# A relative-position table built by 16 shifted transfers, and a 31-tap convolution with all four channel tiles on VectorE

## The chip, the cores and the metric

The kernel runs on one core of a Trainium2 chip. The metric is the device time of one execution in microseconds (us).

## What is computed

Two transformer-like blocks on 256 tokens of width 2048, all float32. The first block has two layers; each projects `x` to 7168 columns, runs three mixers on them (a causal depthwise convolution over 31 taps and 512 channels, a gated recurrence, a retention), projects back, and ends with a feed-forward part of width 8192. The second block has an even layer (neighbourhood attention, a two-way delta rule, attention to a memory) and an odd layer (differential attention). The two places that the change touches are these:

```python
def conv_mixer(a_in, gate_in, w_dw, b_dw, ln_g, ln_b):
    u = a_in.astype(jnp.float32) * jax.nn.sigmoid(gate_in.astype(jnp.float32))
    y = lax.conv_general_dilated(u, w_dw.astype(jnp.float32)[:, None, :], window_strides=(1,),
                                 padding=[(CONV_WIDTH - 1, 0)],
...
                                 feature_group_count=D_CONV) + b_dw
    return jax.nn.silu(layer_norm(y, ln_g, ln_b))

def neighbourhood_attention(q, k, v, rpb):
...
    dr = key_rows - r[:, None] + (NA_WIN_H - 1)
    dc = jnp.clip(c[None, :] - c[:, None], -(NA_WIN_W - 1), NA_WIN_W - 1) + (NA_WIN_W - 1)
    bias = rpb[:, dr[:, None, :, None], dc[None, :, None, :]]
    s = s + bias[None].astype(jnp.float32)
    s = jnp.where(col_ok[None, None, None, :, None, :], s, -jnp.inf)
```

The 256 tokens are a grid of 4 rows by 64 columns, so every query sees all 4 rows and 16 of the 64 columns, and `bias[head, query, key]` depends only on the row difference and the column difference. `rpb` is 6 heads by 15 by 31 numbers.

## The kernel before

**The weight stream.** All big products are units of 512 output columns. A unit is 8 blocks; a block is 256 rows by 512 columns of a weight, 512 KB. For each block SyncE loads it (L221) into one of 8 buffers, ScalarE copies it to a rounded high part `w_hi` (L228), VectorE subtracts to get the low part `w_lo` (L235; called the split below), and TensorE runs 12 matmuls of 128x512 with them (L250 to L252). SyncE loads a block as soon as TensorE has finished the block 8 before it. ScalarE and VectorE run `AHEAD = 6` blocks ahead of TensorE in their program: where TensorE has done n blocks, their text stands behind split n + 6. Position n below means n blocks done in the stage's own count.

**Work woven in.** In a mixer stage each engine's program is written out by hand, `run(n)` standing for the next n blocks of the stream and `upto(run, n)` for all up to position n, with the mixer's own instructions between them. All engines wait for one another through counters (`wait_ge(*k.name.next(who))`, raised by `.then_inc(*k.name.up())`).

**The convolution** (`dve_conv`, `pool_conv`, `pe_conv`, both layers of the first block). Channels lie on partitions in four tiles of 128, 256 tokens along the free axis. VectorE does three tiles: for each tap three multiply-adds of 128x256 (L899), then `run(1)`. It begins at position 5. Behind taps 22, 26 and 27 stand larger steps of the next mixer's gates (`dve_hgrn_gates`, L1086 to L1109), which ScalarE answers with Abs, Exp and Ln (`act_hgrn_gates`). GpSimd does the fourth tile meanwhile, two instructions for a tap (L843, L845), from the time of VectorE's first tap. TensorE transposes the gates' input at position 26 (L935) and, at position 38 in the first layer and 42 in the second, waits for the last tap and for GpSimd, and transposes the result back (L874). VectorE's normalisation and everything later in the mixers follows from that.

**The table** (`pe_even_inputs`, `dve_even_inputs`, even layer). `na_bias` is 128 partitions (two grid rows of 64 query columns) by 6 heads, 2 token tiles, 4 key rows and 64 key columns. TensorE transposes the 90x31 table (L1978) at position 51, and then multiplies it with shifted windows of a constant 31x191 band, 32 products of 31x128 by 42 columns at position 53 and 32 at position 58 (L1993); each picks, for one key column, the entry of every query column. VectorE copies the table (L2069) and moves each half from PSUM to `na_bias`, adding the column mask, in 12 instructions on 64 partitions (L2089). At position 61 it divides (L1849) and scales the heads (L1855), which raises `att_scaled`; TensorE, at position 64, waits for that before it transposes queries and keys (L2118) for the attention. ScalarE squares heads at positions 48 to 58, takes their root, and applies Silu to the gate (L1924). In the attention VectorE adds `na_bias` to the scores of each head (L1774).

`na_bias` shares its SBUF with the delta rule's buffers, which are free once VectorE has raised `dn_scaled` (after L1855 at position 47).

Of the kernel before, what the change touches and what calls it, by code (L numbers as in the profile page):

```python
# [83 lines left out]
def constants():  # L84
# [11 lines left out]
    j, v = np.arange(31)[:, None], np.arange(63 + P)[None, :]  # L96
    band = ((63 - v + 15) % 64 == j).astype(f32)
# [9 lines left out]
        "c_band": band,  # L107
        "c_window": np.concatenate([window, window], 0),
# [540 lines left out]
DVE_CONV = CONV_C // P - 1  # L649
# [11 lines left out]
def first_buffers(k):  # L661
# [43 lines left out]
    k.conv_pool, = count("conv_pool")  # L705
# [117 lines left out]
def pool_conv(pool, k):  # L823

    g = k.nc.gpsimd

    def step(ins):
        ins.then_inc(*k.pool_step.up())
        pool.wait_ge(*k.pool_step.now())

    def weight(n):
        return k.conv_w[:, DVE_CONV, n:n + 1].to_broadcast([P, SEQ])

    y = k.conv_y[:, DVE_CONV, :]
    pool.wait_ge(*k.conv_tap.next("pool"))
    k.conv_tap.next("pool", DVE_CONV * CONV_W - 1)
    step(g.tensor_tensor(y, k.conv_u[:, DVE_CONV, 0:SEQ], weight(0), ALU.mult))
    g.tensor_tensor(k.conv_work[:, 1, :], k.conv_u[:, DVE_CONV, 1:1 + SEQ], weight(1), ALU.mult)
    step(g.tensor_tensor(y, y, weight(CONV_W), ALU.add))
    for tap in range(1, CONV_W):  # L840

        if tap + 1 < CONV_W:
            g.tensor_tensor(k.conv_work[:, (tap + 1) % 2, :], k.conv_u[:, DVE_CONV, tap + 1:tap + 1 + SEQ], weight(tap + 1),  # L843
                            ALU.mult)
        last = g.tensor_tensor(y, y, k.conv_work[:, tap % 2, :], ALU.add)  # L845
        if tap + 1 < CONV_W:
            step(last)
    last.then_inc(*k.conv_pool.up())


def pe_conv(pe, k, l, run):
# [18 lines left out]
    pe.wait_ge(*k.conv_tap.next("pe", DVE_CONV * CONV_W - 1))  # L870
    pe.wait_ge(*k.conv_pool.next("pe"))
# [6 lines left out]
def dve_conv(dve, k, l, run):  # L878
# [514 lines left out]
def second_buffers(k):  # L1393
# [95 lines left out]
    k.att_scaled, k.att_gainT, k.att_gained, k.na_tableT, k.na_table_kept = \  # L1489
        later(DEPTH, k.conv_root, k.conv_linear, k.conv_done, k.h_fT, k.h_f_read)  # L1490
    k.na_toeplitz, k.na_bias_kept, k.att_turned, k.att_turn_kept, k.at_s = \
        later(DEPTH, k.h_kx, k.h_key, k.h_qT, k.h_query, k.h_cumulated)
# [4 lines left out]
    k.dn_summed, = later(DEPTH * DVE_CONV * CONV_W, k.conv_tap)  # L1497
# [253 lines left out]
def dve_attention(dve, k, maps, arrays, run=no_blocks, apart=0):  # L1751
# [15 lines left out]
    for n in range(len(maps) + 2):  # L1767
        run(apart)
        if n < len(maps):
# [3 lines left out]
            if bias is not None:  # L1773
                v.tensor_tensor(att_s[:, n % 2], scores, bias, ALU.add).then_inc(*k.dve_step.up())  # L1774
# [7 lines left out]

def even_maps(k):
# [144 lines left out]
def pe_even_inputs(pe, k, run):  # L1928
# [23 lines left out]
    for part in range(3):  # L1952
# [43 lines left out]
    pe.wait_ge(*k.na_bias_kept.next("pe"))  # L1996
# [1034 lines left out]
```

## Time and profile before

| | |
|---|---|
| time, median of 3 runs | 3681.41 us (3677.53 to 3681.42) |
| profiled execution, its own time | 3684.41 us |
| span of that execution | 3682.5 us |
| TensorE busy | 3506.1 us, 95% |
| VectorE busy | 2214.5 us, 60% |
| ScalarE busy | 1615.8 us, 44% |
| GpSimd busy | 440.9 us, 12% |
| DMA | 615.50 MB, mean 167 GB/s |

The span is from the first to the last instruction that the profiler saw. Busy time is the sum over the engine's instructions, so it says how full an engine is on average and nothing about which wait ends last at one place. In a timeline the start of an instruction minus that of the next is its real pace; its listed duration also holds the part that overlaps with the next one. Brackets give idle time before an instruction and who ended it.

### The profile page before, as it was taken

How to read it: one execution, taken by the hardware profiler on the slowest of the kernel's cores; microseconds unless marked ns; L12 is line 12 of the kernel's file. 1: busy time of each engine (PE TensorE's matmuls, PEld its weight loads, DVE VectorE, ACT ScalarE, POOL GpSimd, SP SyncE). 2: the span in 40 equal slices, each digit the busy share in tenths (PEclk: the TensorE clock that was granted, in tenths of full speed). 3: DMA queues.
4: the chain of work that ended last, by engine and by line, in shares of the span. 5: the costliest groups of instructions: out<-in, count | busy, mean ns of one | idle time of the engine just before them, and what ended most of it. 6: DMA issues, size and time to landing. Idle time of an engine off the chain costs nothing.

```text
span 3682.5 us, 44184 instructions
## 1 busy us (share of the span) xinstructions
PE 3506.1 (95%) x16538; PEld 2929.9 (80%) x16538; DVE 2214.5 (60%) x2397; ACT 1615.8 (44%) x1953; POOL 440.9 (12%) x330
## 2 busy tenths in 40 slices
PE   7899999999999997999999999999999978999999
PEld 6778778887888776877888888888888868788877
DVE  5986565555555688865655555566446553555654
ACT  4454334443434345434444443444445433355553
POOL 0625000000000061340100000000000032000100
PEclk9999999999999999999999999999989889999999
DMA  6545455555555564446656555556645300655544
GB/s 208 171 132 166 172 183 187 191 188 178 188 183 189 170 183 143 137 144 205 217 190 188 192 187 191 189 183 196 194 145 178 109 6 1 194 175 171 177 126 160
DMA packets 310634, 615.50 MB, mean 167 GB/s; under 512 B 19082, under 2 KB 19113, under 8 KB 308539
## 3 DMA queue, kind: packets, MB, share of 16 engines
q1 hardware_dynamic: 306144, 591.73, 50.4%
q0 software_dynamic: 4320, 21.34, 1.7%
q8 instruction: 127, 2.08, 0.2%
q14 instruction: 43, 0.35, 0.0%
HBM read 610.90 MB, written 2.10 MB: 166 GB/s over the span
## 4 chain that ended last, share of the span: by engine, by line
PE 84%; DVE 9%; ACT 2%; DMA 1%; POOL 1%; issue 1%; SPq 0%; DVEq 0%; ACTq 0%; POOLq 0%
PE ps_unit L250 25%; PE ps_unit L252 25%; PE ps_unit L251 25%; DVE sb_w_lo L235 3%; DVE sb_conv_y L899 3%; PE ps_mix L2322 2%; PE ps_mix L973 1%; PE ps_mix L374 1%; PE ps_mix L528 1%; DMA sb_raw<-in_w_in_dram 1%; ACT sb_w_hi L228 1%; PE ps_mix L1993 1%; PE ps_mix L2320 0%; DMA sb_raw<-in_w_ff_dram 0%; PE ps_mix L2677 0%
## 5 line engine op out<-in xcount | busy, mean ns | idle before, releaser
L235 DVE TENSOR_TENSOR sb_w_lo<-sb_raw,sb_w_hi 128x1024 fp32r<-128x1024 f32 x1120 | 1424.8, 1286 | 1028.2 <-ACT sb_w_hi L228 1023.2
L228 ACT ACTIVATE sb_w_hi<-sb_raw 128x1024 fp32r<-128x1024 f32 x1120 | 1177.9, 1059 | 1501.6 <-DMA sb_raw<-in_w_ff_dram 742.9
L250 PE MATMUL ps_unit<-sb_w_hi,sb_a_hi 128*128 128x512 f32 x3456 | 1374.7, 398 | 51.0 <-DVE sb_w_lo L235 27.2
L252 PE MATMUL ps_unit<-sb_w_hi,sb_a_lo 128*128 128x512 f32 x3456 | 1358.0, 393 | 0.0
L251 PE MATMUL ps_unit<-sb_w_lo,sb_a_hi 128*128 128x512 f32 x3456 | 1357.7, 393 | 0.0
L250 PEld LDWEIGHTS ps_unit<-sb_w_hi,sb_a_hi 128*128 128x128 f32 x3456 | 656.5, 190 | 193.7 <-DVE sb_w_lo L235 30.0
L252 PEld LDWEIGHTS ps_unit<-sb_w_hi,sb_a_lo 128*128 128x128 f32 x3456 | 655.6, 190 | 139.2
L251 PEld LDWEIGHTS ps_unit<-sb_w_lo,sb_a_hi 128*128 128x128 f32 x3456 | 656.5, 190 | 132.1
L250 PE MATMUL ps_unit<-sb_w_hi,sb_f_hi 128*128 128x512 f32 x1024 | 400.5, 391 | 0.0
L252 PE MATMUL ps_unit<-sb_w_hi,sb_f_lo 128*128 128x512 f32 x1024 | 399.2, 390 | 0.0
L251 PE MATMUL ps_unit<-sb_w_lo,sb_f_hi 128*128 128x512 f32 x1024 | 398.9, 390 | 0.0
L252 PEld LDWEIGHTS ps_unit<-sb_w_hi,sb_f_lo 128*128 128x128 f32 x1024 | 192.3, 188 | 40.2
L251 PEld LDWEIGHTS ps_unit<-sb_w_lo,sb_f_hi 128*128 128x128 f32 x1024 | 192.4, 188 | 39.5
L250 PEld LDWEIGHTS ps_unit<-sb_w_hi,sb_f_hi 128*128 128x128 f32 x1024 | 192.3, 188 | 39.3
L606 POOL TENSOR_TENSOR sb_relu<-sb_relu 128x1024 f32<-128x1024 f32 x32 | 60.7, 1896 | 1181.6 <-ACT sb_relu L588 1181.6
L358 DVE TENSOR_TENSOR sb_x<-sb_x,ps_unit 128x1024 f32<-128x1024 f32 (+1 forms) x48 | 58.6, 1221 | 109.9 <-PE ps_unit L252 109.9
L899 DVE SCALAR_TENSOR_TENSOR sb_conv_y<-sb_conv_u,sb_conv_w,sb_conv_y 128x256 f32<-128x256 f32 x180 | 112.7, 679 | 0.1
L402 ACT ACTIVATE sb_a_hi<-ps_mix 128x512 fp32r<-128x512 f32 x88 | 50.1, 596 | 127.1 <-PE ps_mix L374 127.0
L414 DVE TENSOR_TENSOR sb_a_lo<-ps_mix,sb_a_hi 128x512 fp32r<-128x512 f32 x88 | 57.6, 686 | 74.1 <-ACT sb_a_hi L402 74.1
L342 ACT ACTIVATE sb_proj<-ps_unit 128x1024 f32<-128x1024 f32 (+1 forms) x48 | 49.2, 1024 | 94.7 <-PE ps_unit L252 94.6
L625 DVE TENSOR_TENSOR sb_f_lo<-ps_mix,sb_f_hi 128x1024 fp32r<-128x1024 f32 x32 | 39.2, 1225 | 42.1 <-ACT sb_f_hi L579 42.1
L362 DVE BATCH_NORM_STATS2 sb_stats<-sb_x 128x6 f32<-128x512 f32 (+1 forms) x96 | 61.8, 685 | 3.0 <-DVE sb_x L358 0.3
(455 smaller groups left out, 2181.4 us busy)
## 6 DMA issues: line engine op xcount, KB each, us to landing
sb_raw<-in_w_ff_dram SPq DMA_DIRECT2D x512, 512.0 KB, 3.6
sb_raw<-in_w_in_dram SPq DMA_DIRECT2D x224, 512.0 KB, 3.6
sb_raw<-in_e_w_in_dram SPq DMA_DIRECT2D x112, 512.0 KB, 3.4
sb_raw<-in_o_w_in_dram SPq DMA_DIRECT2D x112, 512.0 KB, 3.5
sb_raw<-in_w_out_dram SPq DMA_DIRECT2D x64, 512.0 KB, 3.7
sb_raw<-in_e_w_out_dram SPq DMA_DIRECT2D x32, 512.0 KB, 3.7
sb_raw<-in_o_w_out_dram SPq DMA_DIRECT2D x32, 512.0 KB, 3.6
sb_raw<-in_e_w_mem_kv_dram SPq DMA_DIRECT2D x16, 512.0 KB, 3.6
```

The costliest lines, as they stand in the source:

```text
L228: k.nc.scalar.activation(k.w_hi[:, j], k.raw[:, j], ACT.Copy).then_inc(k.hi_ready, 1)
L235: k.nc.vector.tensor_tensor(k.w_lo[:, j], k.raw[:, j], k.w_hi[:, j].bitcast(F32), ALU.subtract).then_inc(k.lo_ready, 1)
L250: k.nc.tensor.matmul(acc, hi[:, kt, tokens], w_hi, start=kt == 0, stop=False)
L251: k.nc.tensor.matmul(acc, hi[:, kt, tokens], w_lo, start=False, stop=False)
L252: last = k.nc.tensor.matmul(acc, lo[:, kt, tokens], w_hi, start=False, stop=kt == KT - 1)
L358: k.nc.vector.tensor_tensor(k.x[:, :, cols], k.x[:, :, cols], k.ps_unit[:, u % 2], ALU.add).then_inc(k.evacuated, BLOCKS)
L362: last = k.nc.vector.bn_stats(k.stats[:, t, bass.ds(chunk, 1), :].rearrange("p c s -> p (c s)"), k.x[:, t, cols])
L402: k.nc.scalar.activation(k.a_hi[:, KB * g:KB * (g + 1), :], k.ps[:, g % 4, :].rearrange("p (a s) -> p a s", a=KB), ACT.Copy).then_inc(*k.t ...
L414: k.nc.vector.tensor_tensor(k.a_lo[:, part, :], k.ps[:, g % 4, :].rearrange("p (a s) -> p a s", a=KB), k.a_hi[:, part, :].bitcast(F32), AL ...
L606: k.nc.gpsimd.tensor_tensor(k.relu2[:, u % 2], k.relu[:, u % 2], k.relu[:, u % 2], ALU.mult).then_inc(k.relu2_ready, 1)
L899: ins = v.scalar_tensor_tensor(y, u, k.conv_w[:, c, tap:tap + 1], y, ALU.mult, ALU.add)
L2322: last = tensor.matmul(out[:, x, :], left[:, n, :], right[:, n, :], start=True, stop=True)
```

## The change

The 64 band matmuls, the transpose and copy of the table and the 24 masked moves out of PSUM are gone. In their place GpSimd issues 16 transfers, one for each token tile, grid row and key row; each writes 64 partitions by 6 heads by 64 columns and reads, for query column q, the 64 numbers that start q places further in a row of the table stored back to front. The key columns so stand in reverse order in `na_bias`; the mask is stored in reverse too, and the attention reads the bias from its last column backwards. VectorE adds the mask in one instruction of 128x3072 elements at position 59. In the convolution GpSimd's part is gone, and VectorE does four multiply-adds for each tap.

```diff
-DVE_CONV = CONV_C // P - 1
+CONV_TILES = CONV_C // P
...
-def pool_conv(pool, k):
...
     pe.wait_ge(*k.h_kx.next("pe"))
-    pe.wait_ge(*k.conv_tap.next("pe", DVE_CONV * CONV_W - 1))
-    pe.wait_ge(*k.conv_pool.next("pe"))
+    pe.wait_ge(*k.conv_tap.next("pe", CONV_TILES * CONV_W - 1))
...
     for tap in range(CONV_W):
-        for c in range(DVE_CONV):
+        for c in range(CONV_TILES):
...
-                dve.wait_ge(sem, done + DVE_CONV * (tap - 1) + c + 1)
+                dve.wait_ge(sem, done + CONV_TILES * (tap - 1) + c + 1)
...
+def from_last_column(bias):
+
+    last = bias[:, :, :, GRID - 1:]
+    return bass.AP(last.tensor, last.offset, [list(step) for step in last.ap[:-1]] + [[-1, GRID]])
...
+NA_BIAS = TT * 2 * GRID_ROWS * 16
+
+
+def pool_na_bias(pool, k):
+
+    rpb = k.dram["na_rpb_2"]
+    pool.wait_ge(*k.dn_scaled.next("pool"))
+    with k.nc.allow_non_contiguous_dma(reason="a window of the table for each query column"):
+        for t in range(TT):
+            for r in range(2):
+                for a in range(GRID_ROWS):
+                    row = WIN_H - 1 - (2 * t + r) + a
+                    src = bass.AP(rpb.tensor, rpb.offset + row * RPB_COLS + WIN_W - GRID,
+                                  [[1, GRID], [RPB_ROWS * RPB_COLS, HEADS], [1, GRID]])
+                    pool.dma_start(k.na_bias[r * GRID:(r + 1) * GRID, :, t, a, :], src).then_inc(*k.na_bias_in.up(16))
...
     tensor.transpose(k.ps[:, 0, 0:4], k.gain_rows[:], k.ident[0:4, 0:4]).then_inc(*k.att_gainT.up())
-    tensor.transpose(k.ps[0:RPB_COLS, 1, 0:HEADS * RPB_ROWS], k.na_rows[:],
-                     k.ident[0:HEADS * RPB_ROWS, 0:HEADS * RPB_ROWS]).then_inc(*k.na_tableT.up())
-    run(2)
...
-            last = tensor.matmul(k.ps[:, n // BIAS_PER_BANK, at:at + BIAS_COLS], pick, table, start=True, stop=True)
-        last.then_inc(*k.na_toeplitz.up())
     run.rest()
-    pe.wait_ge(*k.na_bias_kept.next("pe"))
...
+    run(59 - run.done)
+    dve.wait_ge(*k.na_bias_in.next("dve", NA_BIAS))
+    bias = k.na_bias[:].rearrange("p h t r c -> p (h t r) c")
+    v.tensor_tensor(bias, bias, k.na_window[:].unsqueeze(1).to_broadcast([P, HEADS * SEQ // P * GRID_ROWS, GRID]),
+                    ALU.add).then_inc(*k.na_bias_kept.up())
     run(max(61 - run.done, 0))
...
     g.memset(k.dn_u[:, :, SEQ + 2:DN_T], 0.0).then_inc(*k.dn_pad.up())
+    pool_na_bias(pool, k)
     pool.wait_ge(*k.dn_g_done.next("pool"))
```

Besides these, two of the eleven small loads of `pool_even_rows` are gone (the table and the band), VectorE waits for `na_bias_kept` before the attention, and the table is reversed along its last axis before the launch.

## Rows read from the trace of the kernel before

**Rows 1.** the page, its chain by line: shares of the span
```profile
PE ps_unit L250 25%; PE ps_unit L252 25%; PE ps_unit L251 25%; DVE sb_w_lo L235 3%; DVE sb_conv_y L899 3%; PE ps_mix L2322 2%; PE ps_mix L973 1%; PE ps_mix L374 1%; PE ps_mix L528 1%; DMA sb_raw<-in_w_in_dram 1%; ACT sb_w_hi L228 1%; PE ps_
```

**Rows 2.** chain that ended last, first layer: start us, us, what
```profile
95.05 2.38 DVE sb_conv_y L899 x3
...
97.43 1.69 DVE sb_w_lo L235
```

**Rows 3.** Windows: length, busy PE, PEld, DVE, ACT, POOL, then PEclk, DMA share, GB/s
```profile
91.00:152.00 61.00, 56.17 (x248) 45.05 (x247) 61.00 (x62) 25.14 (x24) 58.65 (x61) 1.00 0.57 173
152.00:172.00 20.00, 20.00 (x91) 16.42 (x90) 20.00 (x31) 1.06 (x1) 0.57 (x1) 1.00 0.61 184
192.00:216.00 24.00, 17.69 (x71) 14.13 (x69) 19.28 (x28) 14.78 (x17) 0.00 (x0) 0.86 0.39 120
...
2506.00:2508.00 2.00, 2.00 (x11) 1.65 (x10) 0.00 (x0) 2.00 (x4) 0.00 (x0) 1.00 1.02 363
2882.00:2887.00 5.00, 5.00 (x14) 3.92 (x14) 4.56 (x9) 0.00 (x0) 0.00 (x0) 0.52 0.00 0
```

**Rows 4.** VectorE timeline, first layer, GpSimd idle: start us, us, line
```profile
157.02 1.27 DVE L899 SCALAR_TENSOR_TENSOR sb_conv_y<-sb_conv_u,sb_conv_w,sb_conv_y 128x256 f32<-128x256 f32 x3
158.21 1.21 DVE L235 TENSOR_TENSOR sb_w_lo<-sb_raw,sb_w_hi 128x1024 fp32r<-128x1024 f32 x1
```

**Rows 5.** VectorE timeline, the second block's five-tap convolution
```profile
2750.26 1.23 DVE L235 TENSOR_TENSOR sb_w_lo<-sb_raw,sb_w_hi 128x1024 fp32r<-128x1024 f32 x1
2751.40 1.68 DVE L2038 SCALAR_TENSOR_TENSOR sb_dn_y<-sb_dn_u,sb_dn_w,sb_dn_y 128x256 f32<-128x256 f32 x4
2752.98 1.23 DVE L235 TENSOR_TENSOR sb_w_lo<-sb_raw,sb_w_hi 128x1024 fp32r<-128x1024 f32 x1
```

**Rows 6.** TensorE timeline, twelve matmuls apart
```profile
87.40 0.39 PE L250 MATMUL ps_unit<-sb_w_hi,sb_a_hi 128*128 128x512 f32 x1
...
90.12 0.39 PE L250 MATMUL ps_unit<-sb_w_hi,sb_a_hi 128*128 128x512 f32 x1
```

**Rows 7.** VectorE timeline, first layer, its waits and the last tap
```profile
174.66 1.23 DVE L235 TENSOR_TENSOR sb_w_lo<-sb_raw,sb_w_hi 128x1024 fp32r<-128x1024 f32 x1 [1.43 <-ACT sb_w_hi L228]
...
181.20 1.23 DVE L235 TENSOR_TENSOR sb_w_lo<-sb_raw,sb_w_hi 128x1024 fp32r<-128x1024 f32 x1 [4.13 <-ACT sb_w_hi L228]
...
197.41 1.27 DVE L899 SCALAR_TENSOR_TENSOR sb_conv_y<-sb_conv_u,sb_conv_w,sb_conv_y 128x256 f32<-128x256 f32 x3
```

**Rows 8.** line L874, the transposes back, both layers: min/median/max ns
```profile
L874 PE MATMUL ps_mix<-sb_square,sb_conv_y x16: 270/347/449, 198.8 to 1440.9; 128*128 128x128 f32 x16
```

**Rows 9.** chain that ended last, around the band matmuls
```profile
2872.34 9.93 PE ps_mix L1993 x64
2898.27 11.78 PE ps_mix L1993 x64
```

**Rows 10.** VectorE timeline, second block, around the table
```profile
2856.92 3.43 DVE L1855 TENSOR_TENSOR sb_proj<-sb_proj,sb_head_ss 128x1536 f32<-128x1536 f32 x2
...
2921.08 0.40 DVE L1849 RECIPROCAL sb_head_ss<-sb_head_ss 128x40 f32<-128x40 f32 x1
...
2927.80 0.69 DVE L1855 TENSOR_TENSOR sb_proj<-sb_proj,sb_head_ss 128x512 f32<-128x512 f32 x1
```

**Rows 11.** ScalarE timeline, gate of the attention, then copies of the stream
```profile
2898.41 1.28 ACT L1924 ACT_TABLE_LOAD   x1
...
2901.10 2.05 ACT L228 ACTIVATE sb_w_hi<-sb_raw 128x1024 fp32r<-128x1024 f32 x2
```

**Rows 12.** DMA queues and issues: KB each, median us to landing
```profile
q1 hardware_dynamic: 306144, 591.73, 50.4%
...
sb_raw<-in_e_w_in_dram SPq DMA_DIRECT2D x112, 512.0 KB, 3.4
...
sb_gain<-in_e_ln_g_dram POOLq DMA_DIRECT2D x1, 1024.0 KB, 7.7
...
sb_gw_raw<-in_e_w_in_dram POOLq DMA_DIRECT2D x1, 192.0 KB, 9.2
```

More of the change, by code:

```diff
@@ L106, in constants @@
         "c_rope": rope.reshape(SEQ, HD),
-        "c_band": band,
-        "c_window": np.concatenate([window, window], 0),
+        "c_window": np.concatenate([window, window], 0)[:, ::-1].copy(),
         "c_pairs": np.ascontiguousarray((lev + lev.transpose(2, 1, 0)).reshape(P, 7 * P)),
@@ L820, in act_conv @@
     a.activation(ca, ca, ACT.Silu).then_inc(*k.conv_done.up())
-def pool_conv(pool, k):
[L825 to L848, printed above, removed]
 def pe_conv(pe, k, l, run):
@@ L1488, in second_buffers @@
     k.gates_kept, k.even_gated = later(DEPTH, k.conv_weights, k.conv_gated)
[L1489 to L1492, printed above, removed]
+    k.att_scaled, k.att_gainT, k.att_gained = later(DEPTH, k.conv_root, k.conv_linear, k.conv_done)
+    k.na_bias_in, = count("na_bias_in")
+    k.na_bias_kept, k.att_turned, k.att_turn_kept, k.at_s = later(DEPTH, k.h_key, k.h_qT, k.h_query, k.h_cumulated)
     k.at_max, k.at_e, k.at_t, k.at_c, k.at_o = later(DEPTH, k.h_o, k.h_square, k.h_msq, k.h_root, k.h_gated)
@@ L1773, in dve_attention @@
             if bias is not None:
-                v.tensor_tensor(att_s[:, n % 2], scores, bias, ALU.add).then_inc(*k.dve_step.up())
+                v.tensor_tensor(att_s[:, n % 2].rearrange("p t (r c) -> p t r c", c=GRID),
+                                scores.rearrange("p t (r c) -> p t r c", c=GRID), bias, ALU.add).then_inc(*k.dve_step.up())
                 scores = att_s[:, n % 2]
@@ L2066, in dve_even_inputs @@
     dve.wait_ge(*k.att_gainT.next("dve"))
-    v.tensor_copy(k.att_gain[:], k.ps[:, 0, 0:4]).then_inc(*k.dve_step.up())
-    dve.wait_ge(*k.na_tableT.next("dve"))
-    v.tensor_copy(k.na_table[:], k.ps[0:RPB_COLS, 1, 0:HEADS * RPB_ROWS]).then_inc(*k.na_table_kept.up())
-    dve.wait_ge(*k.dve_step.now())
+    step(v.tensor_copy(k.att_gain[:], k.ps[:, 0, 0:4]))
     for n in (0, 2):
@@ L2074, in dve_even_inputs @@
     last.then_inc(*k.att_gained.up())
-    run(1)
-    dve.wait_ge(*k.dn_scaled.now())
-    for half in range(2):
-        run(1)
-        dve.wait_ge(*k.na_toeplitz.next("dve"))
-        for first in range(0, BIAS_ROUND, BIAS_PER_BANK):
-            n = min(BIAS_PER_BANK, BIAS_ROUND - first)
-            src = k.ps[:, first // BIAS_PER_BANK, 0:n * BIAS_COLS].rearrange("p (c h a) -> p h a c", c=n, h=HEADS)
-            keys = slice(half * BIAS_ROUND + first, half * BIAS_ROUND + first + n)
-            for t in range(TT):
-                for r in range(2):
-                    part = slice(r * GRID, (r + 1) * GRID)
-                    a = GRID_ROWS - 1 - (2 * t + r)
-                    window = k.na_window[part, keys].unsqueeze(1).unsqueeze(1).to_broadcast([GRID, HEADS, GRID_ROWS, n])
-                    last = v.tensor_tensor(k.na_bias[part, :, t, :, keys], src[part, :, a:a + GRID_ROWS, :], window, ALU.add)
-            run(1)
-        last.then_inc(*k.na_bias_kept.up())
+    run(59 - run.done)
[3 more added lines that the diff above has]
+                    ALU.add).then_inc(*k.na_bias_kept.up())
     run(max(61 - run.done, 0))
@@ L2143, in dve_even_attention @@
     dve.wait_ge(*k.even_gated.next("dve"))
+    dve.wait_ge(*k.na_bias_kept.now())
     dve_attention(dve, k, even_maps(k), k.e_att)
```

34 lines of the change are left out of this document (6 added, 28 removed).

## The prediction

> **What bounds the kernel now.** I read the chain by line first, then the chain in order of time at both places of the change, then the timelines of single engines there and the windows over them, last the DMA issues. The chain by line: half and more of it is the three matmul lines of the weight stream, and two VectorE lines follow, the split L235 and the convolution's L899 [rows 1]. So the kernel is bound by TensorE, except where something holds it up, and both edits are at such places. TensorE's own pace is 2.72 us a block: 87.40 to 90.12 for twelve matmuls [rows 6].
>
> In the convolution the chain runs through VectorE: 2.38 us for the three tiles of a tap and 1.69 for the split, 4.07 us a block [rows 2]. While that lasts GpSimd is busy for 58.65 of 61 us; from 152 on it does nothing but 0.57 us of its last tap [rows 3], and VectorE's same three multiply-adds take 158.21 - 157.02 = 1.19 us [rows 4], half of before. The split beside an idle GpSimd takes 2751.40 - 2750.26 = 1.14 [rows 5]. GpSimd's two-input instructions hold VectorE's two-input ones back, and for 15 blocks (61 us / 4.07) this sets VectorE's pace. TensorE lives on its lead of 6 blocks meanwhile and hardly idles (56.17 of 61 busy), but at the transposes back it waits for the last tap, which ends at 198.6 [rows 7], and L874 starts at 198.8 [rows 8].
>
> In the even layer the band matmuls stand on the chain with 9.93 and 11.78 us [rows 9]. TensorE is its own bound there: it does them instead of the stream.
>
> **Part 1, the convolution.** Four multiply-adds and a split are in the trace already: the five-tap convolution of the second block does just that, with GpSimd idle, from split to split 2752.98 - 2750.26 = 2.72 us [rows 5]. It is TensorE's pace to the hundredth, so VectorE neither gains nor loses on it. Along VectorE's program in layer 1:
> - 15 blocks at 2.72 instead of 4.07: 20.2 us earlier.
> - 14 later blocks with a fourth multiply-add of 1.19 / 3 = 0.40: 5.6 later; one more at tap 0: 0.4 later.
> - VectorE idles before two splits for ScalarE's gate work (1.43 and 4.13 us [rows 7]). ScalarE starts that when VectorE's L1087 is done, so it moves along; the fourth multiply-add lies inside the idle, 0.8 back.
>
> That makes 15.0, the last tap at 183.6. Can TensorE be there? It is at position 5 at 87.4 [rows 6]. 33 blocks at 2.72 are 89.8, and the gates' 12 transposes with their wait some 3 us (the 8 of L874 are of 0.27 to 0.35 us each [rows 8]): position 38 at 180.2. So it waits 3.4 us for the tap, less than now, and VectorE stays the bound. Its lag behind TensorE stays under the six blocks. What follows L874 is a chain of its own (normalise, root, Silu, scan) and moves as it is.
>
> Layer 2 has the same 15 slow blocks and the same steps of ScalarE behind VectorE's, so its transposes back, now at 1440.9 [rows 8], move by 15.0 too.
>
> One more term has only bounds. In 192 to 216 TensorE idles 6.3 of 24 us, and its granted clock is 0.86 in the mean, so part of the stretch at 1.2 GHz and not at 2.4 [rows 3]; with a shorter idle the clock may stay up, worth 0 to 24 x 0.14 = 3.4 us a layer. I take 1 each. Part 1: 15 + 15 + 2 = 32 us, range 25 to 38. GpSimd's own edit costs nothing: its next work waits for VectorE's scan, and its DMAs at the stage's head stand ahead of it as before.
>
> **Part 2, TensorE's side of the table.** The first band product starts at 2872.34, two blocks after position 51 [rows 9], so position 51 is at 2866.9 and, with 13 blocks straight, position 64 at 2866.9 + 35.4 = 2902.3. Now it comes at 2928.5: 26 us, of which 21.7 are the products and most of the rest the clock: behind them, 2882 to 2887, it is granted at 0.52, that is 1.2 GHz, with 14 matmuls where 2.72 / 12 each would give 22 [rows 3].
>
> **VectorE's side.** TensorE needs `att_scaled`, raised now at the end of the scaling, 2928.4 [rows 10]. A load lands 3.4 us after its issue [rows 12], then come 1.03 for ScalarE's copy (2.05 for two [rows 11]) and 1.14 for the split; split n + 6 is issued when TensorE is at n - 2. So VectorE reaches position 59 when TensorE is at 57 (2883.2) plus 5.6, at 2888.8; ScalarE's Silu with its table load (2901.10 - 2898.41 = 2.7 [rows 11]) falls there and pushes the copy by 1.8, as the squares before it leave ScalarE little room: 2890.6. Then the mask, 3072 elements: by the scaling's L1855, 3.43 for two of 1536 [rows 10], 3.4 us. Two splits 2.3: 2896.3. From divide to `att_scaled` is 2921.08 to 2928.4 now, 7.3 [rows 10]: 2903.6. That is behind TensorE's 2902.3, so the gain is 2928.4 - 2903.6 = 24.8. The attention then reads the bias backwards; no row has a negative step. I take 0; at half speed it would be 6 heads x 0.6 = 3.6.
>
> **The 16 transfers** are what the trace doesn't price. They may start when `dn_scaled` is up (2856.92 + 3.4 = 2860.3 [rows 10]) and are wanted at 2890.6, 30 us. Each has 384 runs of 256 bytes, 6144 in all. Lower bound, by bytes: 1.5 MB, about 1.5 of the 1 MB `gain` broadcast at 7.7 us [rows 12], under 12 us. Upper bound, each run as dear as a packet of the stream: 50.4% of 3682.5 us x 16 engines over 306144 packets is 97 ns [rows 12]; 384 runs for each engine are 37 us, in the 0.4 of the engines that the stream leaves 93 us, 62 late. Nearest row: `gw_raw`, 2048 runs of 96 bytes, lands after 9.2 us although it is queued behind that broadcast [rows 12]; three of it are 27.6, ending at 2888. I take that they are just in time. They push the stream too: in 2506 to 2508 the engines are full [rows 3]. TensorE has six blocks of lead against that, VectorE's position 59 doesn't; 2 us off. Part 2: 24.8 - 2 = 23 us, range 8 to 27.
>
> The page "DMA: Bandwidth & Descriptors" of the Trainium skill (Specifications) asks for at least 512 bytes in a run for full rate, and its fixed cost (Anatomy of one DMA) is about 2.0 us plus bytes / 436e3 per transfer. Sixteen of 98 KB one after another would by that be an estimated 36 us, 6 late, and the gain of part 2 some 17 instead of 23; `gw_raw`'s row stands against it only if they overlap, which no row here shows.
>
> **Sum.** 32 + 23 = 55. Against the profiled execution: span 3682.5 - 55 = 3627, own time 3684.4 - 55 = 3629. The median of the runs is 3.0 below that own time: 3626.
>
> **The rivals.**
> - *Transfers late, still a gain.* VectorE stands at position 59; the path from there to `att_scaled` is serial, so each us late is one lost. For: runs of 256 bytes, a full DMA system. Against: `gw_raw`. 10 to 40 late: a gain of 15 to 45, about 3650.
> - *Slower than before.* The same wait, with the transfers one after another, each as long as `gw_raw` (9.2 us): 147 us, done at 3008, 117 late, so 3681 - 55 + 117 = 3743. It decides from (30.3 + 55) / 16 = 5.3 us a transfer. Everything is behind it, since VectorE's splits wait too and TensorE starves after six blocks. Against: four small loads of the trace don't add up like that.
> - *The convolution gives little.* If VectorE's slowness were not GpSimd's doing, four tiles would take 4.07 + 0.80 = 4.87 a block and each layer lose. Against: the step to 1.19 falls where GpSimd stops, in both layers. A milder form: TensorE or ScalarE comes late at the transposes and half of the 30 us is lost, 3641.
>
> **Chances.** Forecast (gain 42 to 68) 0.68; late transfers with a gain 0.15; half the convolution 0.10; slower 0.05; no effect that shows 0.02. From no change a measurement of this kernel can tell about 0.2%, 7 us. So faster 0.93, same 0.02, slower 0.05. The range takes the forecast's own spread (sum of the parts' bounds, 3616 to 3648) and a little of the late case above it: 3612 to 3652.
>
> **What would show it.** After tap 0, L899 at 1.59 us for four and the split at 1.13, 2.72 a block from the first tap on, L874 near 184; no L1993, and the clock full from 2866 on in old time; the mask instruction of 3072 elements with no idle for a DMA before it; `att_scaled` some 37 us after position 51. The prediction is wrong if VectorE idles for `na_bias`, if the split's idle for ScalarE grows by more than a block in the convolution, or if the stream's loads land late while the 16 are in flight.

## The result, and the profile after

The changed kernel's median is 3625.77 us (four runs, 3622.23 to 3627.62) beside 3681.38 for the kernel before: a ratio of 0.9846, 95% interval 0.9835 to 0.9858. The prediction was 3626.0, in the range 3612 to 3652. The profiled execution took 3622.23 us by its own time, span 3620.4. Its line numbers differ from those of before: the split is L232 (was L235), ScalarE's copy L225 (L228), the convolution L865 (L899), the transposes back L840 (L874), the first products behind them L939 (L973), the scaling L1835 (L1855), the mask L2037, the 16 transfers L1789.

The page's chain by line answers to [rows 1]; the split and the convolution have gone from 3% each to 2%. The band matmuls are no longer in the program:

```profile
PE ps_unit L247 26%; PE ps_unit L249 26%; PE ps_unit L248 26%; DVE sb_w_lo L232 2%; PE ps_mix L2271 2%; DVE sb_conv_y L865 2%; PE ps_mix L939 1%; PE ps_mix L371 1%; PE ps_mix L525 1%; DMA sb_raw<-in_w_in_dram 1%; ACT sb_w_hi L225 1%; PE ps_mix L2269 0%; DMA sb_raw<-in_e_w_in_dram 0%; PE ps_mix L2626 0%; PE ps_mix L2606 0%
```

**The convolution.** VectorE's timeline in the first layer (start us, us, line), against [rows 2] and [rows 4]:

```profile
103.57 1.23 DVE L232 TENSOR_TENSOR sb_w_lo<-sb_raw,sb_w_hi 128x1024 fp32r<-128x1024 f32 x1
104.71 1.68 DVE L865 SCALAR_TENSOR_TENSOR sb_conv_y<-sb_conv_u,sb_conv_w,sb_conv_y 128x256 f32<-128x256 f32 x4
106.29 1.23 DVE L232 TENSOR_TENSOR sb_w_lo<-sb_raw,sb_w_hi 128x1024 fp32r<-128x1024 f32 x1
107.42 1.68 DVE L865 SCALAR_TENSOR_TENSOR sb_conv_y<-sb_conv_u,sb_conv_w,sb_conv_y 128x256 f32<-128x256 f32 x4
...
157.00 1.23 DVE L232 TENSOR_TENSOR sb_w_lo<-sb_raw,sb_w_hi 128x1024 fp32r<-128x1024 f32 x1 [1.04 <-ACT sb_w_hi L225]
...
163.55 1.22 DVE L232 TENSOR_TENSOR sb_w_lo<-sb_raw,sb_w_hi 128x1024 fp32r<-128x1024 f32 x1 [3.74 <-ACT sb_w_hi L225]
```

From tap to tap it is 107.42 - 104.71 = 2.71 us, where it was 4.07: one multiply-add more, and both lines at their quick pace. The two idle times for ScalarE were 1.43 and 4.13 [rows 7]; each is 0.39 shorter, since one multiply-add more lies inside it.

The windows of the same stretches, and those around the 16 transfers (length, busy PE, PEld, DVE, ACT, POOL, granted clock, DMA share, GB/s), answer to [rows 3]:

```profile
91.00:152.00 61.00, 61.00 (x277) 50.67 (x276) 60.74 (x111) 26.33 (x25) 0.00 (x0) 1.00 0.65 190
152.00:172.00 20.00, 20.00 (x90) 16.57 (x89) 15.18 (x24) 15.00 (x13) 0.00 (x0) 1.00 0.66 186
172.00:192.00 20.00, 14.85 (x64) 12.24 (x63) 19.86 (x31) 7.54 (x8) 0.00 (x0) 0.91 0.42 128
192.00:216.00 24.00, 22.45 (x116) 18.63 (x116) 20.29 (x16) 17.16 (x18) 8.68 (x4) 1.00 0.53 154
2820.00:2828.00 8.00, 8.00 (x37) 6.36 (x36) 4.17 (x4) 7.16 (x33) 8.00 (x13) 1.00 0.93 244
2828.00:2836.00 8.00, 8.00 (x37) 6.64 (x36) 1.91 (x5) 3.60 (x13) 1.97 (x4) 1.00 1.04 256
2836.00:2844.00 8.00, 8.00 (x37) 6.64 (x36) 4.63 (x4) 7.90 (x33) 0.00 (x0) 1.00 0.77 250
```

GpSimd is out of the first stretch, and TensorE does 277 matmuls in it where it did 248. The transposes back, line L840 over both layers, answer to [rows 8] (its columns are min/median/max ns, then the first and the last start); the second fence is TensorE's timeline at the first of them:

```profile
L840 PE MATMUL ps_mix<-sb_square,sb_conv_y x16: 270/347/445, 183.6 to 1404.8; 128*128 128x128 f32 x16
```

```profile
183.58 0.66 PE L840 MATMUL ps_mix<-sb_square,sb_conv_y 128*128 128x128 f32 x2 [5.15 <-DVE sb_conv_y L865]
```

So 198.8 became 183.6 and 1440.9 became 1404.8, and TensorE still waits 5.15 us there for the last tap.

**The table.** VectorE's timeline around it, against [rows 10]:

```profile
2815.93 3.43 DVE L1835 TENSOR_TENSOR sb_proj<-sb_proj,sb_head_ss 128x1536 f32<-128x1536 f32 x2
2819.28 1.22 DVE L232 TENSOR_TENSOR sb_w_lo<-sb_raw,sb_w_hi 128x1024 fp32r<-128x1024 f32 x1
...
2851.40 1.23 DVE L232 TENSOR_TENSOR sb_w_lo<-sb_raw,sb_w_hi 128x1024 fp32r<-128x1024 f32 x1 [2.73 <-ACT sb_w_hi L225]
2852.54 3.35 DVE L2037 TENSOR_TENSOR sb_na_bias<-sb_na_bias,sb_na_window 128x3072 f32<-128x3072 f32 x1
...
2858.08 0.40 DVE L1829 RECIPROCAL sb_head_ss<-sb_head_ss 128x40 f32<-128x40 f32 x1
...
2864.80 0.69 DVE L1835 TENSOR_TENSOR sb_proj<-sb_proj,sb_head_ss 128x512 f32<-128x512 f32 x1
2865.40 2.35 DVE L232 TENSOR_TENSOR sb_w_lo<-sb_raw,sb_w_hi 128x1024 fp32r<-128x1024 f32 x2
2867.67 2.06 DVE L2085 TENSOR_SCALAR sb_na_t<-ps_mix,sb_att_gain 128x512 f32<-128x512 f32 x3
```

The instruction behind the scaling shows when `dn_scaled` is up, 2819.3, and when `att_scaled` is up, 2865.4. That is 46.1 us, where it was 2928.4 - 2860.3 = 68.1 [rows 10]. The mask has no bracket in front: it waits for no transfer. The transfers themselves, line L1789 (issue durations in ns, first and last start, then issue to landing), and the queues from 2815 to 2860:

```profile
L1789 POOL DMA_DIRECT2D sb_na_bias<-in_na_rpb_dram x16: 653/656/697, 2819.7 to 2829.3; - x16
...
DMA to landing us min/median/max: 3.7/5.9/7.1
```

```profile
q1 hardware_dynamic: 4380, 8.44, 62.2%
q0 software_dynamic: 768, 1.57, 15.6%
...
sb_raw<-in_e_w_in_dram SPq DMA_DIRECT2D x9, 512.0 KB, 5.4
```

They are issued 0.64 us apart and all have landed by 2829.3 + 7.1 = 2836.4, 16 us ahead of the mask. On the 16 engines they take 15.6% of 45 us, 7.0 us of each engine. The stream pays some of it: for some 16 us the DMA engines are full (shares of 0.93 and 1.04) and its loads take 5.4 us to land instead of 3.4 [rows 12]. TensorE goes on without a gap in all three windows.

### The profile page after: what moved, and what is told of

It reads as the page before. It is cut to its first block, busy times and chain, and to the rows that moved or that the text cites. A ratio compares the mean times of both kernels' runs of the same rounds, so it can differ in the third digit from the quotient of the medians.

```text
span 3620.4 us, 43852 instructions
## 1 busy us (share of the span) xinstructions
PE 3467.1 (96%) x16409; PEld 2901.0 (80%) x16409; DVE 2176.0 (60%) x2435; ACT 1619.0 (45%) x1953; POOL 329.4 (9%) x220
## 4 chain that ended last, share of the span: by engine, by line
PE 86%; DVE 8%; ACT 2%; DMA 1%; POOL 1%; issue 1%; SPq 0%; DVEq 0%; ACTq 0%; POOLq 0%
PE ps_unit L247 26%; PE ps_unit L249 26%; PE ps_unit L248 26%; DVE sb_w_lo L232 2%; PE ps_mix L2271 2%; DVE sb_conv_y L865 2%; PE ps_mix L939 1%; PE ps_mix L371 1%; PE ps_mix L525 1%; DMA sb_raw<-in_w_in_dram 1%; ACT sb_w_hi L225 1%; PE ps_mix L2269 0%; DMA sb_raw<-in_e_w_in_dram 0%; PE ps_mix L2626 0%; PE ps_mix L2606 0%
## 5 line engine op out<-in xcount | busy, mean ns | idle before, releaser
L232 DVE TENSOR_TENSOR sb_w_lo<-sb_raw,sb_w_hi 128x1024 fp32r<-128x1024 f32 x1120 | 1406.6, 1268 | 1046.0 <-ACT sb_w_hi L225 1041.0
L225 ACT ACTIVATE sb_w_hi<-sb_raw 128x1024 fp32r<-128x1024 f32 x1120 | 1178.2, 1059 | 1479.2 <-DMA sb_raw<-in_w_ff_dram 741.7
L399 ACT ACTIVATE sb_a_hi<-ps_mix 128x512 fp32r<-128x512 f32 x88 | 50.4, 596 | 126.7 <-PE ps_mix L371 126.7
L865 DVE SCALAR_TENSOR_TENSOR sb_conv_y<-sb_conv_u,sb_conv_w,sb_conv_y 128x256 f32<-128x256 f32 x240 | 100.8, 492 | 0.1
L1022 POOL TENSOR_TENSOR sb_h_d<-sb_h_cum 128x768 f32<-128x768 f32 x16 | 33.0, 2063 | 353.8 <-DVE sb_h_cum L1102 260.9
```

What stands on the lines that cost most here:

```text
L225: k.nc.scalar.activation(k.w_hi[:, j], k.raw[:, j], ACT.Copy).then_inc(k.hi_ready, 1)
L232: k.nc.vector.tensor_tensor(k.w_lo[:, j], k.raw[:, j], k.w_hi[:, j].bitcast(F32), ALU.subtract).then_inc(k.lo_ready, 1)
L399: k.nc.scalar.activation(k.a_hi[:, KB * g:KB * (g + 1), :], k.ps[:, g % 4, :].rearrange("p (a s) -> p a s", a=KB), ACT.Copy).then_inc(*k.t ...
```

## Experiments

### The two parts, one at a time

The convolution of the changed kernel with the table of the kernel before, and the reverse. The core of each diff, against the kernel before:

```diff
 e1_conv_only
-        for c in range(DVE_CONV):
+        for c in range(CONV_TILES):
-def pool_conv(pool, k):
 e2_table_only
+    pool_na_bias(pool, k)
+    run(59 - run.done)
+    dve.wait_ge(*k.na_bias_in.next("dve", NA_BIAS))
```

> The kernel before with the convolution's edit alone (four tiles on VectorE, nothing on GpSimd), the table still by band products. The prediction's part 1: 32 us faster, 3649, with L874's place near 184 in the first layer and 15 us earlier within the second. Rival, that the table's edit carries most of it and the convolution gives half: 15 us, 3666.

> The kernel before with the table's edit alone, three tiles on VectorE and one on GpSimd as before. By the trace of after, part 2 is 22 us (scaled heads 46 us after the delta rule's scaling instead of 68): 3659. If the two parts only add up by luck of the executions, this and the convolution's alone don't sum to the 56 of the whole; if they are independent they do within the intervals.

The convolution alone: 3647.83 us, ratio 0.9912 (0.9897 to 0.9928), 31.2 us under the 3679.06 of the kernel before in the same set of runs. The table alone: 3659.82, ratio 0.9955 (0.9941 to 0.9969), 19.2 under it. The transposes back, by line, in these two kernels (L843 in the first, L871 in the second):

```profile
L843 PE MATMUL ps_mix<-sb_square,sb_conv_y x16: 270/286/421, 183.9 to 1406.5; 128*128 128x128 f32 x16
```

```profile
L871 PE MATMUL ps_mix<-sb_square,sb_conv_y x16: 270/339/417, 197.6 to 1434.7; 128*128 128x128 f32 x16
```

The first has them where the changed kernel has them, the second near where the kernel before had them (198.8 and 1440.9). Its second ones are 6.2 us earlier, though it has the old convolution and nothing is changed in front of them: so much can one execution differ from another by itself. 31.2 + 19.2 = 50.4 accounts for most of the 52 to 56 that both together give, so nothing shows that the parts touch each other. The ratios, which come from the same runs, put the two gains at 32.4 and 16.6 us; the intervals are 26.5 to 37.9 and 11.4 to 21.7.

### Is it GpSimd's reading that slows VectorE?

Two kernels that add GpSimd work beside VectorE's taps in the changed kernel. In the first GpSimd does 31 multiplies that read the convolution's fourth tile and 30 adds that read a scratch tile; all write the scratch tile and all have two inputs. In the second it only writes: 120 fills of 128x512.

```diff
 e3_pool_reads
+            g.tensor_tensor(work(tap + 1), k.conv_u[:, 3, tap + 1:tap + 1 + SEQ], weight(tap + 1), ALU.mult)
+        last = g.tensor_tensor(work(tap), work(tap), work(tap), ALU.add)
 e4_pool_writes
+    for n in range(120):
+        last = k.nc.gpsimd.memset(k.conv_work[:], 0.0)
```

> The changed kernel, with GpSimd again doing two instructions of 128x256 for each tap that read SBUF, on a scratch buffer that nobody uses (work added). Theory, GpSimd's reads hold VectorE back: four multiply-adds 3.2 us and the split 1.7, about 4.9 us a block while GpSimd works, at least 25 us a layer slower than the changed kernel, some 3680 to 3700. Rival, the wait was the fourth tile's being elsewhere and the semaphores between the engines: VectorE keeps its 2.72 a block and the time stays at 3626.

> The changed kernel, with GpSimd doing 120 memsets of 128x512 beside the taps, which write SBUF and read none (work added). If only reads of SBUF hold VectorE's two-input instructions, VectorE keeps 2.72 us a block and the time is 3626; if any GpSimd instruction does, the block is longer by the same share as with reads.

With reads it was 3674.73 us, with writes 3629.91. VectorE's timeline with reads:

```profile
100.11 1.63 DVE L232 TENSOR_TENSOR sb_w_lo<-sb_raw,sb_w_hi 128x1024 fp32r<-128x1024 f32 x1
101.67 3.09 DVE L895 SCALAR_TENSOR_TENSOR sb_conv_y<-sb_conv_u,sb_conv_w,sb_conv_y 128x256 f32<-128x256 f32 x4
104.68 1.63 DVE L232 TENSOR_TENSOR sb_w_lo<-sb_raw,sb_w_hi 128x1024 fp32r<-128x1024 f32 x1
```

and with writes:

```profile
98.87 1.21 DVE L232 TENSOR_TENSOR sb_w_lo<-sb_raw,sb_w_hi 128x1024 fp32r<-128x1024 f32 x1
100.00 1.66 DVE L880 SCALAR_TENSOR_TENSOR sb_conv_y<-sb_conv_u,sb_conv_w,sb_conv_y 128x256 f32<-128x256 f32 x4
101.59 1.21 DVE L232 TENSOR_TENSOR sb_w_lo<-sb_raw,sb_w_hi 128x1024 fp32r<-128x1024 f32 x1
```

Their windows from 91 to 151, reads first:

```profile
91.00:151.00 60.00, 51.50 (x221) 40.59 (x220) 60.00 (x71) 21.84 (x21) 52.22 (x60) 1.00 0.54 160
```

```profile
91.00:151.00 60.00, 60.00 (x272) 49.84 (x271) 60.00 (x111) 26.35 (x25) 54.08 (x104) 1.00 0.64 189
```

GpSimd is busy to the same share in both (52.2 and 54.1 of 60 us). With reads a block takes 104.68 - 100.11 = 4.57 us: four multiply-adds 3.01 instead of 1.59, the split 1.56 instead of 1.13. With writes it stays at 2.72. So GpSimd's being busy doesn't slow VectorE; its two-input instructions, which read SBUF, do. (The two kernels also differ in the kind of GpSimd instruction, and none has an instruction with one input; the reads are what the two sets of instructions differ in by design.) The size fits too: GpSimd ends at 145.6 us, so 12 blocks are 1.85 longer, 22 us, and with the slower tap 0 the first transposes back start at 206.6, 23.0 later than in the changed kernel. Two layers make 46; measured, in one run against the 3626.88 of another set, 47.9.

The page "SBUF — State Buffer" of the Trainium skill says the same of who is hit ("SBUF: two separate sides": a VectorE instruction with two SBUF inputs contends only with a GpSimd instruction that reads SBUF), and both runs agree. It also says that the loser is blocked for the whole instruction of the other. The run with reads shows less: GpSimd starts 5 instructions in a block that is 1.85 longer, so 0.37 us for each, where the shortest is recorded with 0.68 us. One after another, VectorE's 2.72 and GpSimd's 5 x 0.68 would take 6.1 us, and the block takes 4.57.

### Does the fourth tile cost anything?

```diff
 e6_three_tiles
-CONV_TILES = CONV_C // P
+CONV_TILES = 3
+    k.nc.gpsimd.memset(k.conv_y[:, 3, :], 0.0).then_inc(*k.conv_pool.up())
```

> Leaves out the taps of the fourth channel tile (it is filled with zeros once by GpSimd, outside the taps), so VectorE has 3 taps and a split in a block: 1.19 + 1.13 = 2.32 us, and GpSimd reads nothing beside it. My theory: in the changed kernel VectorE (2.72 us a block) and TensorE (12 matmuls, 2.72) are level, so taking the fourth tile away moves nothing but the 5.1 us wait in front of the transposes back in the first layer: 3620 to 3626, windows of the stretch 91:152 with PE at 60 of 61 us and DVE near 52. If VectorE alone set the pace, 31 blocks of two layers would each be 0.4 us shorter, 25 us: 3602. If the gain of the change had come from anything but GpSimd's reads, this kernel, whose VectorE does just what it did before the change, would stay at 4.07 us a block: about 3658.

It took 3624.68 us in a single run, inside the 3622 to 3631 of the changed kernel's. VectorE's timeline:

```profile
99.76 1.22 DVE L232 TENSOR_TENSOR sb_w_lo<-sb_raw,sb_w_hi 128x1024 fp32r<-128x1024 f32 x1
100.89 1.27 DVE L875 SCALAR_TENSOR_TENSOR sb_conv_y<-sb_conv_u,sb_conv_w,sb_conv_y 128x256 f32<-128x256 f32 x3
102.65 1.23 DVE L232 TENSOR_TENSOR sb_w_lo<-sb_raw,sb_w_hi 128x1024 fp32r<-128x1024 f32 x1 [0.49 <-ACT sb_w_hi L225]
...
110.84 1.22 DVE L232 TENSOR_TENSOR sb_w_lo<-sb_raw,sb_w_hi 128x1024 fp32r<-128x1024 f32 x1 [0.47 <-ACT sb_w_hi L225]
```

The four blocks from 99.76 to 110.84 take 11.08 / 4 = 2.77 us each, though VectorE has only 2.32 us of work in one: it waits for ScalarE's copies, and these come at TensorE's pace. The fourth tile fills what would be idle time. VectorE's convolution here is the one of the kernel before, three tiles and a split, and without GpSimd beside it it no longer takes 4.07 us a block: a second sign that GpSimd's part was the cause. The transposes back did come earlier, at 180.1 and not 183.6; whether those 3.5 us reach the end a single run can't tell, but the 25 us of the rival are excluded.

### The transfers one after another, and as shorter runs

In `e5_in_series` GpSimd waits for each transfer's landing before it issues the next. In `e9_short_runs` each transfer is cut in two by columns, so there are 32 with runs of 128 bytes, 12288 runs in all.

```diff
 e5_in_series
+                    if (t, r, a) != (0, 0, 0):
+                        pool.wait_ge(*k.na_bias_in.next("pool", 16))
 e9_short_runs
+                    for c in (0, GRID // 2):
-                                  [[1, GRID], [RPB_ROWS * RPB_COLS, HEADS], [1, GRID]])
+                                      [[1, GRID], [RPB_ROWS * RPB_COLS, HEADS], [1, GRID // 2]])
```

> The changed kernel with the 16 transfers one after another, each issued when the one before has landed. This gives the time of one such transfer alone, which the forecast bounded between 0.7 and 9.2 us, and tests the path behind them: by the rival's working each us that they end after VectorE's position 59 (33 us after their start) costs one. At 3 us each, 48 us: 15 late, less 2 for the stream that is no longer pushed, 3639. At the page's estimated 2.2 us, 36: 3 late, 3627.

> The same table by 32 transfers of half the columns: twice as many issues and runs, each of 128 bytes, the same bytes; all the work is done. Theory: the issue (0.64 us each on GpSimd's queue) sets the time, so 32 take 20.5 us and the last lands about 2819.7 + 20.5 + 6 = 2846, ahead of the mask at 2852.5: no wait and 3622 to 3628. If the price is by run and they share the engines with the weight stream so that the landing doubles to 12 us or more, the mask waits a few us for the DMA and the stream's transfers take longer than the 5.4 us median: 3630 to 3640.

In series: 3651.14 us. The transfers' line and then VectorE's timeline at the mask:

```profile
L1791 POOL DMA_DIRECT2D sb_na_bias<-in_na_rpb_dram x16: 648/648/697, 2824.2 to 2880.6; - x16
...
DMA to landing us min/median/max: 2.7/3.4/4.7
```

```profile
2883.45 3.36 DVE L2039 TENSOR_TENSOR sb_na_bias<-sb_na_bias,sb_na_window 128x3072 f32<-128x3072 f32 x1 [28.92 <-DMA sb_na_bias<-in_na_rpb_dram]
```

From issue to issue it is (2880.6 - 2824.2) / 15 = 3.76 us. The last three intervals, when TensorE stands still and the weight stream with it, are 3.1 us each, with about 2.9 us to the landing. VectorE waits 28.9 us for the table, and the kernel is 24.3 us slower than the changed one of the same set. The difference between the two is mostly what the 16 cost when they are in flight together: here VectorE stands at the mask 2883.45 - 28.92 - 2824.2 = 30.3 us after the first issue, where in the three traces of the changed kernel it gets there after 32.4 to 34.2. In the trace of the same set it is 34.2, so 28.9 - 3.9 = 25.0 us net: each microsecond that the table is late is lost, as the rival had it. The breakpoint worked out was 5.3 us a transfer; 3.76 stays under it, so even in series the change would have been a gain, 28.2 us in this single run. I had the loss too small in both expectations.

Shorter runs: 3628.55 us, again a single run. Its transfers' line, then its queues from 2815 to 2865:

```profile
L1790 POOL DMA_DIRECT2D sb_na_bias<-in_na_rpb_dram x32: 658/737/821, 2825.9 to 2845.8; - x32
...
DMA to landing us min/median/max: 3.2/4.3/5.3
```

```profile
q0 software_dynamic: 1024, 1.57, 18.6%
```

The issue sets the time: (2845.8 - 2825.9) / 31 = 0.64 us, as before. The mask waits for no transfer. On the engines they take 18.6% of 50 us, 9.3 us of each. With half as many runs it was 7.0, and 6.6 to 7.7 in all the traces that have the 16 transfers in flight together. So twice the runs cost 20 to 40% more and not twice, and a run of 256 bytes costs 7.0 / 384 = 18 ns with its bytes, against the 97 that the prediction held as its upper bound. That bound took a run for a packet, and the profile doesn't count them so: it has 768 packets for the 6144 runs, and 1024 for the 12288. The time on the engines is no fixed price either: one after another the same 768 packets took 14.4% of 60 us (2824 to 2884), 8.6 us.

### The two waits that are left

`e7_mask_early` puts the mask at VectorE's position 56 instead of 59, so that the divide can go at 59. `e8_late_both` uses in both layers the later positions that so far only the second layer has. `e10_both` has both edits.

```diff
 e7_mask_early
-    run(59 - run.done)
+    run(56 - run.done)
-    run(max(61 - run.done, 0))
+    run(59 - run.done)
 e8_late_both
-    upto(run, 38 + LATE * l)
+    upto(run, 38 + LATE)
```

(The second edit in all 19 places that have this term.)

> The changed kernel once more, as the mark for the other kernels of this call: 3626, ratio 0.985.

> The changed kernel with VectorE's mask instruction at position 56 instead of 59 and the divide and scaling at 59 instead of 61. The trace of after has TensorE idle 4.3 us before the attention's transposes, waiting for the scaled heads, with 2.7, 0.9 and 1.8 us of VectorE's idle between positions 56 and 59 and two splits (2.3) between 59 and 61. Theory, that this wait is made of VectorE's order alone: the heads are scaled about 5 us earlier, the idle goes, 4 us faster than the changed kernel (3622). Rival, that the transfers are not in by position 56: VectorE would wait for them there and the time stays.

> The changed kernel, with the positions that the second layer already has (four later from the transposes back on) in the first layer too. TensorE idles 5.15 us at position 38 there for the last tap. If that idle is lost time, four blocks in front of the transposes fill it and the kernel is 5 us faster (3621); if what follows the transposes is a chain of its own that TensorE then waits for with fewer blocks to fill it, it is no faster (3626), or slower by up to 5.

> The mask moved three VectorE units ahead and both LATE positions made equal in the two layers, in one kernel; all the work is done. Each of the two edits alone had a median about 3 us under the changed kernel (3623.5 and 3623.8 against 3626.9), less than their intervals are wide. If both are real and apart from each other, this one is at 3620 to 3621. If each only fills one idle stretch that another wait then takes (in the profile of the early mask TensorE's 4.3 us for att_scaled went to 0.3 but a wait of 6.7 for na_t came in its place), it is at 3623 to 3627, no different from the changed kernel.

> The changed kernel as it is, as the mark for the kernel beside it: 3622 to 3628, as in its nine runs so far.

| kernel | median us | ratio to before, 95% interval |
|---|---|---|
| changed, again | 3626.88 | 0.9862 (0.9845 to 0.9878) |
| mask early | 3623.53 | 0.9852 (0.9835 to 0.9868) |
| late in both layers | 3623.79 | 0.9851 (0.9835 to 0.9868) |
| changed, a third time | 3628.38 | 0.9857 (0.9842 to 0.9872) |
| both edits | 3619.57 | 0.9836 (0.9823 to 0.9850) |

The first three rows are of one set of runs on one chip, the last two of another. The line of the transposes back with both edits, and its windows at the same place:

```profile
L840 PE MATMUL ps_mix<-sb_square,sb_conv_y x16: 270/272/275, 188.1 to 1402.4; 128*128 128x128 f32 x16
```

```profile
172.00:192.00 20.00, 20.00 (x94) 16.62 (x94) 19.01 (x26) 11.39 (x11) 0.00 (x0) 1.00 0.64 194
```

Four blocks of the stream, 10.9 us, now stand ahead of the transposes, and these start 188.1 - 183.6 = 4.5 us later with no wait in front. The stretch that had TensorE busy for 14.85 of 20 us at a granted clock of 0.91 has it busy throughout at 1.00. How much of that remains by the second layer's transposes these traces can't tell: both edits have them at 1402.4, the later positions alone at 1401.8, and the three traces of the changed kernel at 1404.8, 1406.7 and 1403.4. At the table, TensorE's timeline with the mask early shows what came in place of the 4.33 us that it waited for `att_scaled`:

```profile
2864.56 1.96 PE L2065 MATMUL ps_mix<-sb_square,sb_proj 128*128 128x128 f32 x16 [0.25 <-DVE sb_proj L1835]
2869.76 3.48 PE L2065 MATMUL ps_mix<-sb_square,sb_proj 128*128 128x128 f32 x16 [3.24 <-DVE sb_na_t L2085]
```

TensorE starts on time, fills its banks and waits there, as VectorE still has four splits to do (4.62 us) before it empties them. From the first transfer's issue to the first emptying it is 2868.96 - 2822.7 = 46.3 us with the mask early and 49.3 in the changed kernel of the same set, and 2863.24 - 2818.9 = 44.3 with both edits against 47.5: 3.0 and 3.2 us less.

Each edit alone is under what these runs can tell. Both together are 8.8 us under the changed kernel of the same set, some 0.2%; the intervals overlap by 0.0008, so that this version beats the changed kernel is likely, and not settled. Of these 8.8 the traces show 3.2 at the table. What the later positions give is within the 3.3 us by which the changed kernel's own traces differ.

## Why the prediction was right

**The pace of the convolution.** Predicted 1.59 + 1.13, 2.72 a block, read off the second block's convolution [rows 5]; measured just that, from the first taps on. In the stretch of [rows 3] VectorE waits once, 0.26 us for ScalarE's copy, and TensorE has no gap. The runs with reads, with writes and with three tiles show the cause, which the prediction had argued from where GpSimd stops: GpSimd's two-input instructions.

**The last tap.** Predicted at 183.6; L840 starts at 183.58. TensorE is at position 38 at 183.58 - 5.15 = 178.4, where 180.2 was worked out: I gave the gates' transposes and their wait 3 us; the twelve took 1.48 us with no wait (144.26, L901). So the wait is 5.15 and not 3.4, which costs nothing by itself: VectorE was the bound there in both.

**The second layer.** Its transposes came 1440.9 - 1404.8 = 36.1 us earlier. When that stage begins the changed kernel is 21.0 ahead already (1253.00 to 1232.03 for the same instruction), so the layer gave 15.1, as the first (198.8 - 183.6 = 15.2).

**The clock.** I took 1 us a layer out of 0 to 3.4, and this term is the weak one: it came out, in part by luck. The windows of 192 to 216 can't be set side by side, since the same work stands 15 us earlier in the changed kernel. From the transposes back to the first product of L973 or L939, before and after, the rows are:

```profile
198.80:227.20 28.40, 26.85 (x117) 21.93 (x117) 23.57 (x23) 14.91 (x17) 7.62 (x4) 0.91 0.44 127
```

```profile
183.60:211.00 27.40, 25.85 (x117) 21.22 (x117) 23.55 (x23) 13.58 (x15) 7.66 (x4) 0.95 0.45 132
```

So the first layer gained 1.0 more there (16.2 in all, 227.18 to 210.94), at a granted clock of 0.95 where it was 0.91. TensorE had stood idle for 6.24 us before the transposes in the kernel before, and 5.15 in the changed one. But a second trace of the changed kernel has 28.4 us and 0.91 in this stretch, a third 27.3 and 0.95, and the kernel with the table's edit alone, which has the old convolution, 27.6 and 0.94. The clock's share differs by 1 us from execution to execution, so no run shows that the change brought it. In the second layer the first of these products gained 0.9 more than the transposes (1472.24 to 1435.24), the last one 1.6 (1477.2 to 1439.5, so 16.7 in all). Sum of part 1 by this pair of traces: 16.2 + 16.7 = 32.9, predicted 32; by the runs of that part alone 31.2.

**The table.** The worked-out path was `dn_scaled` to the mask 30.3 + 2, measured 2852.54 - 2819.3 = 33.2 (in the series run, whose transfers hardly push the stream, 2854.53 - 2823.8 = 30.7); mask 3.4, measured 3.35; `att_scaled` at 43.3 + 2 = 45.3, measured 46.1. So the gain is 68.1 - 46.1 = 22.0 by the trace, predicted 23, and 19.2 by the runs of that part alone, whose interval (11.4 to 21.7 us) ends just below both. The trace of that part alone has 46.5 us for this path, a gain of 21.6. TensorE then waits 4.33 us for `att_scaled` (3.7 to 5.6 in the three traces) and not 1.3 plus the 2.

**The step that was off: the transfers.** "I take that they are just in time" was wrong in size: they were 16 us early. The nearest row, `gw_raw` at 9.2 us for 2048 runs, was read as if its time went by its runs. What the runs showed: in flight together the 16 go by their issue, 0.64 us each, and the last lands at most 7.1 us behind its own. The error cost the forecast nothing, since a transfer that is early is as good as one just in time; but the 0.15 and 0.05 given to the late rivals rested on it. The 2 us set aside for the stream were about right (2.1 to 3.9, the 32.4 to 34.2 us above against the series run's 30.3), and came through where I said: VectorE's splits wait 3.67 and 3.14 us for ScalarE, with loads at 5.4 us. The prediction also named late loads of the stream as a sign that it was wrong. That sign was set too sharp: the loads were late, 5.4 us in the median and up to 9.1 where 3.4 was usual, and that cost VectorE's path about what had been set aside and TensorE nothing, which has no gap in the three windows around the transfers. The other two signs, VectorE idle for `na_bias` and a longer idle for ScalarE in the convolution, didn't appear.

The estimate by the page "DMA: Bandwidth & Descriptors" of the Trainium skill (Anatomy of one DMA) was 36 us for the 16 one after another, 2.25 each. The series run took 3.76 each, of which 3.4 to the landing, 2883.45 - 2824.2 = 59 us in all. The Trainium skill's fit is too low for these runs of 256 bytes, beside the stream and also without it (3.1 each, 2.9 to the landing). In flight together they took 2836.4 - 2819.7 = 16.7.

**Reading backwards.** The addition of the bias to the scores before, and then with the negative step (min/median/max ns):

```profile
L1774 DVE TENSOR_TENSOR sb_e_att_s<-ps_mix,sb_na_bias x6: 691/692/692, 2938.7 to 2952.3; 128x512 f32<-128x512 f32 x6
```

```profile
L1733 DVE TENSOR_TENSOR sb_e_att_s<-ps_mix,sb_na_bias x6: 680/692/692, 2875.4 to 2887.9; 128x512 f32<-128x512 f32 x6
```

The step is free, as taken.

**The rivals.** "The convolution gives little" fell with the pace of 2.72 and with the 31.2 us of that part alone. "Late, still a gain" did not happen by itself, but the series run made it: 28.9 us of waiting, 24.3 lost. "Slower" needs 5.3 us a transfer; not even a full wait between transfers comes to that.

**What stays open.** The profiled pair differs by 62.1 us of span, of which the three stages explain 16.2 + 16.7 + 22.0 = 54.9. The other 7 us lie in the stretches between, 4.8 of them (21.0 - 16.2) between the two layers. The medians differ by 55.6, and the other traces show that single executions differ by as much: between L973's or L939's first product and the second layer the profile of before takes 1025.8 us, the kernel with the table's edit alone, which has the same program there, 1022.1, and the three traces of the changed kernel 1020.6 to 1022.9. In the kernel with the table's edit alone `dn_scaled` is up 8.7 us earlier than before (2851.6 against 2860.3), with only two small loads gone in front of it. So the pair of profiles overstates the gain, and the medians are the better figure. Why executions differ so is open. The two parts alone add up to 50.4 and both together give 52 to 56: within the intervals.

## What to carry to other kernels

Weigh work given to a second engine by what it does to the first: three tiles and a split took VectorE 4.07 us beside GpSimd's reads and would take 1.19 + 1.13 = 2.32 alone, so the fourth tile on GpSimd cost VectorE 1.75 us a block, where doing it itself costs 0.40. An instruction of one shape with two durations is the sign to look for, with what the other engines do while it has the longer one. Many small transfers can take a table's building off the busiest engine if they are issued together and far enough ahead: 17 us here, but 59 when each waited for the one before. And set traces of the same kernel side by side before giving a microsecond here or there to an edit: here they differ by 3 us and more at one and the same instruction.

## What of the hardware had not been expected

- GpSimd fills of 128x512, which only write, don't touch VectorE's pace at all (2.72 us a block, GpSimd busy for 54.08 of 60 us). GpSimd's two-input instructions of 128x256 back to back make a VectorE multiply-add of 128x256 take 0.75 us instead of 0.40, and a split of 128x1024 1.56 instead of 1.13.
- A transfer of 96 KB in 384 runs of 256 bytes takes 3.4 us from issue to landing when no other of its kind is in flight, 2.9 when the weight stream stands still too, and 5.0 to 6.7, by the median of a trace, when 16 are issued together; the issue takes 0.65 to 0.70 us of GpSimd either way.
- Cut into runs of 128 bytes, with the same bytes, the 16 transfers took 9.3 us on each DMA engine (one run) where they had taken 6.6 to 7.7: less than twice as much for twice the runs.
